# Hybrid decoder step: two gate projections spread over experts 2 to 7, and tile 1's memory steps placed one expert later

## What is computed

```python
proj = xn @ w_in
q, k, v, gu, gv = jnp.split(proj, [Q_END, K_END, V_END, GU_END], axis=-1)
gu = jax.nn.gelu(gu, approximate=False)
sgu = gu * mixed(gv)                       # spatial gate over chunks of 128
merged = jnp.concatenate([rms_norm(attn), rms_norm(sgu)], axis=-1)
x = x + merged @ w_out
x = x + memory_attention(rms_norm(x), mem_k, mem_v, w_cq, w_co)

def block(xt):                             # 128 tokens, 8 heads, 16 experts per head
    q = (xt @ w_pq).reshape(128, 8, 2, 128)
    s = jnp.einsum('thcd,hckd->thck', q, sub_keys)
    ...                                    # top 16 of each half, top 16 of the sums
    h = jnp.einsum('td,thkd->thk', xt, u_tab[idx])
    a = gelu(h) * gate
    return jnp.einsum('thk,thkd->td', a, v_tab[idx])
```

## Time and profile before

| | |
|---|---|
| median of 3 runs | 1698.52 us (1696.72 to 1699.43) |
| profiled execution, time | 1697.96 us |
| its span | 1696.2 us |
| PE busy | 1307.6 us, 77% |
| DVE busy | 1165.1 us, 69% |
| ACT busy | 806.8 us, 48% |
| POOL busy | 656.4 us, 39% |
| read from HBM | 653.24 MB, 388 GB/s over the span |

### The profile page before, as it was taken

The page is one execution under the profiler, slowest core; times in us unless marked ns, Lnnn a source line. Parts: engine busy times, 40 slices in busy tenths (PEclk is TensorE's granted clock), DMA queues, the critical chain, the costliest instruction groups (busy, mean ns, idle before and its releaser), DMA issues.

```text
span 1696.2 us, 21662 instructions
## 1 busy us (share of the span) xinstructions
PE 1307.6 (77%) x7069; PEld 474.2 (28%) x7069; DVE 1165.1 (69%) x2798; ACT 806.8 (48%) x2337; POOL 656.4 (39%) x584
## 2 busy tenths in 40 slices
PE   9998987877888777678787776777677677766776
PEld 4454442333344222123232111212112111111110
DVE  2545749797667676777777677677666676777764
ACT  1424456774445454455555454445444445444443
POOL 0000234434534344444444444444444444444441
PEclk9999998989999788988988777877878877788865
DMA  9426799999999999999999999999999999999995
GB/s 359 165 100 251 274 388 420 414 374 421 420 421 421 417 394 414 422 405 412 421 420 421 421 421 421 421 422 420 421 421 422 421 406 421 422 421 420 421 418 220
DMA packets 97441, 657.88 MB, mean 388 GB/s; under 512 B 12512, under 2 KB 15584, under 8 KB 20768
## 3 DMA queue, kind: packets, MB, share of 16 engines
q0 software_dynamic: 83056, 604.28, 86.3%
q1 hardware_dynamic: 14272, 52.21, 8.0%
HBM read 653.24 MB, written 4.19 MB: 388 GB/s over the span
## 4 chain that ended last, share of the span: by engine, by line
DMA 44%; PE 25%; DVE 12%; ACT 11%; issue 7%; POOL 1%; ACTq 0%; DVEq 0%; POOLq 0%
DMA R<-in_peer_uv,R 42%; PE ps L2118 9%; PE ps L1624 5%; DVE R L1543 5%; PE ps L1878 3%; ACT L954 2%; ACT R L963 2%; ACT R L958 1%; PE ps L1595 1%; DVE R L1331 1%; ACT R L954 1%; DVE R L1332 1%; DVE R L1334 1%; ACT L862 1%; POOL R L684 1%
## 5 line engine op out<-in xcount | busy, mean ns | idle before, releaser
L2118 PE MATMUL ps<-R 64*64 64x512 f32 x4528 | 741.5, 736 | 355.8 <-ACT R L963 355.6
L684 POOL DMA_INDIRECT R<-in_peer_uv,R x566 | 643.6, 1137 | 830.7 <-PE ps L2118 754.1
L1543 DVE CUSTOM_DVE_ANT_0 R<-R 128x1024 f32<-128x1024 f32 x566 | 687.8, 1224 | 374.1 <-DMA R<-in_peer_uv,R 370.3
L954 ACT ACTIVATE R<-R 128x1 f32<-128x1 f32 x576 | 115.8, 201 | 602.0 <-DVE R L1543 600.7
L2118 PEld LDWEIGHTS ps<-R 64*64 64x64 f32 x4528 | 136.4, 151 | 710.2 <-ACT R L963 624.2
L963 ACT ACTIVATE R<-R 128x64 f32<-128x64 f32 x576 | 200.4, 348 | 54.9 <-ACT R L958 1.9
L1878 PE MATMUL ps<-A,R 128*128 128x256 f32 (+1 forms) x640 | 221.0, 470 | 0.7 <-ACT R L839 0.7
L958 ACT ACTIVATE R<-R 128x1 f32<-128x1 f32 x576 | 169.7, 295 | 20.9
L1878 PEld LDWEIGHTS ps<-A,R 128*128 128x128 f32 (+1 forms) x640 | 94.8, 198 | 256.1 <-issue 253.1
L1624 PE MATMUL ps<-A,R 128*128 128x512 f32 (+1 forms) x256 | 100.7, 545 | 0.4 <-ACT R L735 0.4
L1595 PE MATMUL ps<-R 128*128 128x256 f32 (+2 forms) x352 | 79.8, 382 | 0.0
(11 more groups left out here) (304 smaller groups left out, 947.5 us busy)
## 6 DMA issues: line engine op xcount, KB each, us to landing
R<-in_peer_uv,R POOLq DMA_INDIRECT x566, 15.6
A<-in_w_pq SPq DMA_DIRECT2D x8, 1024.0 KB, 9.8
A<-in_w_in SPq DMA_DIRECT2D x3, 2048.0 KB, 20.2
R<-in_w_out SPq DMA_DIRECT2D x4, 1024.0 KB, 9.0
x_res<-in_x_prompt SPq DMA_DIRECT2D x6, 512.0 KB, 8.6
R<-in_w_out_rows SPq DMA_DIRECT2D x1, 3072.0 KB, 9.9
R<-in_x_promptT SPq DMA_DIRECT2D x4, 512.0 KB, 7.3
R<-in_w_cq SPq DMA_DIRECT2D x2, 1024.0 KB, 10.7
```

Source lines behind the costliest of these rows:

```text
L684: pool.indirect_dma_start(slots[slot_of[g]], None, I["peer_uv"][:, :], bass.IndirectOffsetOnAxis(ap=idx[:, b % 4, k:k + 1], axis=0)).then_ ...
L954: act.activation(hgelu[:, b % 2, col], hdot[:, b % 2, col], ACT.Gelu).then_inc(gelu_ready, 1)
L1543: dve.tensor_tensor_reduce(u, u, xn(t), 1.0, 0.0, ALU.mult, ALU.add, hdot[:, b % 2, k:k + 1]).then_inc(u_used, 1)
L2118: ins = pe.matmul(bank(2 * (t % 2) + q)[rows], diag[tokens, g % DIAGS, :], v_rows[slot_of[g]][tokens, c * 512:(c + 1) * 512], start=first, ...
```

## The change

On PE, `project(3, 2)` is cut into two pieces, five contraction steps ahead of expert 2 and three ahead of expert 3. `project(4, 2)` was cut into five and three steps ahead of experts 4 and 5; it is now three, three and two, ahead of experts 5, 6 and 7. `gating(4)` goes from expert 6 to 8, `heads_T(3)` from 8 to 10, `heads_T(4)` from 10 to 11, `half_T(3)` from 11 to 12. `half_T(4)` stays ahead of expert 13, but has a bank of its own and no longer waits for `half_take(3)`. On ACT, `gates_out(3)` and `gates_out(4)` go from 2 and 6 to 3 and 7, `qkT_evac(3)` from 9 to 10, and both `half_norm` from 8 to 10, now behind `qkT_evac(3)`. On DVE, `gated(3)` goes from 3 to 4, `gated(4)` from 7 to 9, `half_rows` from 9 to 11, the two `half_take` from 12 and 13 to 13 and 14. All of tile 1's memory steps (`prep`, query, `cross`, `ffn`) move one expert later on every engine.

```diff
-        PREP_AT = {1: 1, 2: 122, 3: 200, 4: 210}
-        QUERY_AT = {1: 6, 2: 134, 3: 208, 4: 218}
-        CROSS_AT = {1: 9, 2: 138, 3: 222, 4: 244}
-        FFN_AT = {1: 28, 2: 158, 3: 268, 4: 16 * 23 + 2}
+        PREP_AT = {1: 2, 2: 122, 3: 200, 4: 210}
+        QUERY_AT = {1: 7, 2: 134, 3: 208, 4: 218}
+        CROSS_AT = {1: 10, 2: 138, 3: 222, 4: 244}
+        FFN_AT = {1: 29, 2: 158, 3: 268, 4: 16 * 23 + 2}
...
-            return 1 if t <= 2 else 5
+            return 1 if t <= 2 else 5 if t == 3 else 3
...
-                    if g == 8:
+                    if g == 10:
+                        qkT_evac(3)
                         half_norm(3)
                         half_norm(4)
...
-                elif g == 7:
-                    gated(4)
                 elif g == 9:
+                    gated(4)
...
                 elif g == 2:
                     pe.wait_ge(x1_out, 2)
-                    project(3, 2)
-                elif g == 4:
+                    project(3, 2, 0, 5)
+                elif g == 3:
+                    project(3, 2, 5, KD)
+                elif g == 5:
                     pe.wait_ge(sgu_out, 4)
-                    project(4, 2, 0, 5)
-                elif g == 5:
-                    project(4, 2, 5, KD)
+                    project(4, 2, 0, 3)
                 elif g == 6:
+                    project(4, 2, 3, 6)
+                elif g == 7:
+                    project(4, 2, 6, KD)
+                elif g == 8:
                     pe.wait_ge(pq_so, 2)
                     gating(4, bank(5))
```

More of the change, by code:

```diff
@@ L989, in _ @@
                     diagonal(b, k)
-                    if g == 2:
+                    if g == 3:
                         gates_out(3)
-                    if g == 6:
+                    if g == 7:
                         gates_out(4)
-                    if g == 8:
+                    if g == 10:
+                        qkT_evac(3)
                         half_norm(3)
                         half_norm(4)
-                    if g == 9:
-                        qkT_evac(3)
                     if g == 11:
@@ L1415, in beside @@
                     add_one()
-                elif g == 3:
+                elif g == 4:
                     gated(3)
-                elif g == 7:
+                elif g == 9:
                     gated(4)
-                elif g == 9:
+                elif g == 11:
                     half_rows(3)
                     half_rows(4)
-                elif g == 12:
+                elif g == 13:
                     half_take(3)
-                elif g == 13:
+                elif g == 14:
                     half_take(4)
@@ L1668, in half_T @@
                 pe.wait_ge(h_rows, t)
-                if t > 1:
+                if t in (2, 3):
                     pe.wait_ge(h_T, t - 1)
@@ L1940, in beside @@
                     pe.wait_ge(x1_out, 2)
-                    project(3, 2)
-                elif g == 4:
+                    project(3, 2, 0, 5)
+                elif g == 3:
+                    project(3, 2, 5, KD)
+                elif g == 5:
                     pe.wait_ge(sgu_out, 4)
-                    project(4, 2, 0, 5)
-                elif g == 5:
-                    project(4, 2, 5, KD)
+                    project(4, 2, 0, 3)
                 elif g == 6:
+                    project(4, 2, 3, 6)
+                elif g == 7:
+                    project(4, 2, 6, KD)
+                elif g == 8:
                     pe.wait_ge(pq_so, 2)
                     gating(4, bank(5))
-                elif g == 8:
+                elif g == 10:
                     pe.wait_ge(p_T, 3)
@@ L1953, in beside @@
                     heads_T(3)
-                elif g == 10:
+                elif g == 11:
                     pe.wait_ge(qkT_out, 8)
                     heads_T(4)
-                elif g == 11:
+                elif g == 12:
                     pe.wait_ge(qkT_out, 10)
@@ L1962, in beside @@
                 elif g == 14:
-                    pe.wait_ge(h_T, 4)
+                    pe.wait_ge(h_T, 3)
                 elif g == 16:
```

## The result

The changed kernel is slower. Its median is 1705.22 us (1703.45 to 1709.99, 6 runs) against 1698.33 us (1696.72 to 1701.47, 6 runs) for the kernel before; the ratio is 1.0045, 95% interval 1.003 to 1.006. The forecast was 1696.3 with a range up to 1702.0, so the time lies outside it and on the other side of no change. The profiled execution took 1706.9 us, its span 1705.1.

The account below looks back on a forecast made before the run. DMA was taken as the bound, with a ceiling of 4.9 us lost from 200 to 240. Earlier gathers less later loads and norms gave 2.2 us, memory steps 0: 1697.96 - 2.2 = 1695.8, median 1696.3, range 1692.8 to 1702.0.

Parts of the forecast that it names:

- The pieces: PE, experts 2 to 8: projections cut in pieces free slots sooner, so gather 10 is issued 4.3 us earlier.
- The stop at `gated(3)`: PE, `project(4, 2)`: its new wait for DVE's `gated(3)` costs 0, with 1.0 us as its bound.
- The loads behind the last projection: SP's loads for heads 2 and 6: issued some 4.3 us later, alone on the DMA from 220, landed at 225.1.
- My own test for a wrong forecast: PE ahead of `q_mm(2)`: an idle time of over 3 us would show the forecast wrong.
- the first rival: Loads for heads 2 and 6 land late, holding PE until 231.4; 4.1 us slower, 1702.6; chance 0.14.
- The price of that wait: PE's wait for the loads for heads 2 and 6: each microsecond delays gather 17, priced 1 for 1.
- the forecast's own queue: DMA behind gather 17: three gathers, 7.5 us, and SP's loads, 4.4, follow; gather 20 lands at 252.4 to 253.5.
- The second of my signs for a wrong forecast: DMA: a landing of gather 20 after 255 would show the forecast wrong; it was expected near 253.
- The norms ahead of expert 11: ACT's norms behind `heads_T(3)` make PE idle 3.5 us; expert 11 runs at 233.7 against 233.06 before.
- The memory steps one expert later: Tile 1's later norm makes DVE wait about 1.7 us ahead of L1305; priced at 0, 1.7 without cover.
- My sign for it: DMA: a dip of the rate behind 290 that wasn't there before would show the forecast wrong.
- The sum: Gather 20 lands 1.6 to 2.7 us earlier than 255.1; 2.2 us taken as the whole gain, median 1696.3.

Follow-up runs that it names:

- e2: The changed kernel with both `half_norm` on ACT one expert earlier, ahead of expert 10's diagonal and `qkT_evac(3)`; ratio to the kernel before 0.9998 (0.9983 to 1.0013).
- e7: The kernel before with only tile 1's `ffn` one expert later, at 29 instead of 28; ratio to the kernel before 1.0014 (1.0003 to 1.0024).
- e4: The changed kernel with half block 2's query product one expert later, its first piece behind expert 10; ratio to the kernel before 1.0014 (0.9996 to 1.0032).
- e6: The changed kernel with tile 1's `cross` back at expert 9 and `ffn` left at 29; ratio to the kernel before 1.0022 (1.0011 to 1.0032).
- e5: The changed kernel with `cross` and `ffn` back at 9 and 28 and both `half_norm` ahead of expert 10; ratio to the kernel before 1.0002 (0.9990 to 1.0014).
- e11: e5 with the last `w_pq` piece (head 7) loaded as soon as `gating(4)` is done; ratio to the kernel before 0.9990 (0.9978 to 1.0002).
- e1: The changed kernel with tile 1's `cross` and `ffn` back at experts 9 and 28; ratio to the kernel before 1.0004 (0.9984 to 1.0024).
- e10: e2 with tile 1's `ffn` back at expert 28, `cross` left at 10; ratio to the kernel before 1.0022 (1.0007 to 1.0036).
- e9: The changed kernel with tile 1's `ffn` back at expert 28, `cross` left at 10; ratio to the kernel before 1.0040 (1.0025 to 1.0054).
- e12: The kernel before with only the last `w_pq` piece (head 7) loaded early, behind heads 2 and 6; ratio to the kernel before 0.9979 (0.9967 to 0.9991).

## Why the prediction was wrong, point by point

**The pieces: right.** Expert 4 started at 205.05 (forecast 205.3), expert 6 at 212.64 (212.9), expert 8 at 222.09 (222.6), gather 10 was issued at 206.45 (206.7). The stop at `gated(3)`, priced at 0, cost 0: `project(4, 2)` at 206.07 has no idle time in front. The rate near 400 came only in 200 to 210 (422); in 210 to 220 it was 324.

**The loads behind the last projection: the first step that failed.** I had the gathers done at 220, the DMA free for the loads from there, and both landed at 225.1, 7.3 us after the later issue. The last two gathers needed 3.6 and 4.2 us instead of 2.5, the second in part beside the first load, so gather 12 landed at 222.72; the loads took 7.4 and 9.5, and PE went on at 227.49, 2.4 us late. Why the rate fell to 324 GB/s with gathers queued no run here shows. My own test for a wrong forecast, an idle of over 3 us ahead of `q_mm(2)`, was met with 3.45. This is the first rival's mechanism, at the very landing time, 9.5, from which I had said it decides; I had given it 0.14. The fit that I had quoted from the Trainium skill, page "DMA: Bandwidth & Descriptors", section "Anatomy of one DMA — SWDGE (gpsimd) path", gave an estimate of 6.8 us for both, and this trace shows 9.9 from the first issue to the later landing (9.5 from its own issue).

**The price of that wait: wrong too.** I had counted one microsecond of delay as one microsecond of loss. By that, 2.4 us would have cancelled the gain of 2.2 and ended at no change. But `q_mm(2)` and `cross` also ran at half clock: 1.66 + 2.08 instead of the 1.08 and 1.13 us that such pieces take at the full clock, 1.5 us more. That alone isn't the loss either: e2 has the wait and the slow pieces and no early loss. It is one for one and more only because ACT's block and expert 11 stand behind them. Then the forecast's own queue was gone. I had gather 18 lined up behind 17; in fact it was issued at 245.35, 4.9 us behind it, and gather 20's dot started at 259.67, where I had a landing of 252.4 to 253.5. From a common start that is some 7 us between forecast and fact: expert 10 4.7 us late, and the rest, some 2 us, behind gather 17, with which no gather was queued; that split is read from the rows, not tested. The second of my signs for a wrong forecast, a landing of gather 20 after 255, came true as well.

**The norms ahead of expert 11: right in mechanism and size.** Forecast was an idle time of 3.5 us; it was 3.56. The first activation behind the table load for expert 11 starts 1.29 us after that load (235.90, 237.19). On page "ScalarE: Activation LUTs", section "What ACT_TABLE_LOAD costs", the Trainium skill adds a drain of 1.38 us to each load; the trace again shows none. Expert 11 then took 1.98 us, half clock, as I had allowed for. What the runs add is that this block is harmful only in series with the wait: e2 keeps the wait of 3.3 us, lets the norms run in it, and has no early loss.

**The memory steps one expert later: the second step that failed.** I priced them at 0, with 1.7 as the cost without cover. DVE's wait was 1.58 us, as foreseen, and the lag of the dots grew by 2.1 at expert 32, while the gathers went on landing with a lag of 5.5 up to expert 43. The cover lay from expert 44 on, in dots that wait for their gathers, and can hide only what hasn't reached the gathers by then. It had: `unit`'s exponentials on ACT were as late as the dots (by 7.5 us), PE's transposes behind them by 10.1, gather 45 was issued 9.6 late, where gather 44 was 6.3 late, and from expert 48 the gathers land 9.5 late. The step from 7.5 to 10.1 is the one consumer I hadn't followed at all: `unit`'s transposes on PE wait for the second half that ACT takes for `ffn` at L907. Moving `ffn` past one expert put a table load and three activations ahead of it, and PE waited 5.65 us instead of 2.95. Alone, the place of `ffn` costs 2.4 us (e7). My sign for it, a dip behind 290 that wasn't there before, came true: 361 GB/s from 320 to 340, where the kernel before has 420.

**The sum.** The early part ends 4.8 us behind where I had 2.2 ahead, the late part adds some 4 of lag. That makes 9 of lag, as the spans say too (1705.1 against 1696.2), and 6.9 us of median time. The other 2 are the choice of the profiled executions: the changed kernel's lies 1.7 us over its median, the one before 0.4 under. The same holds for e2, whose lag at the end is still 3.2 at a ratio of 0.9998: the execution that it is held against lies 2.8 us under the median of the kernel before in e2's round. Open is the size of the early loss in time: e2 and e4, which take it away and leave the rest, lie 8.0 and 5.3 us under the changed kernel by the ratios, 4.9 and 2.9 by the plain medians. Open too is why the last gathers ahead of the loads were slow.

## What to carry to other kernels

A load that is issued when a step ends moves with that step, and its landing time depends on what it then meets. When a change pulls the main traffic forward, list every load issued in the next 30 us with its consumer, and give each the slowest landing that the trace shows for it; here a SyncE load of 1 MB took 5.7 (e4) to 16.3 us. A step moved by one place must be followed to all who wait for its outputs, on every engine, also those whose own place is fixed. And a wait costs little if other work can run in it and much if a block on another engine stands behind it in series, so look for the block first. The one edit that paid, an independent load put where the engines had room, needed no change of the order at all.

## What the runs showed of the hardware

A wait of 1.06 to 2.10 us on PE ahead of `q_mm(2)` (e6, e5, e11, e1, e10) left its first piece at 1.08 us, the full clock. A wait of 3.22 to 3.45 us (e9, e2, the changed kernel) was followed by 1.98, 1.42 and 1.66 us; in the changed kernel `cross` then took 2.08 us at a granted clock of 0.50, 1.2 GHz. The last wait alone doesn't tell it: behind the same two waits, 1.5 and 1.15 us, expert 9 took 1.09 us in the kernel before and 1.98 in e7 and e12.

The load of the last `w_pq` piece, 1 MB on SyncE, took 9.4 to 10.4 us when at most one gather was in flight at its issue (e1, e4, e6, the changed kernel), 11.9 with two (e2), and 16.3 with two or three and the next ones close behind (e5, the kernel before). I had taken it that the two loads had the engines to themselves "from 220 on"; the gathers ahead of them ended at 222.72, and the loads landed 2.3 us later than I had them. Gather 17 of the changed kernel, issued with nothing in flight, took 5.6 us to land, as long as the 5.5 of the earlier trace rows.
